# A hybrid attention and recurrence block: the output written feature by feature from the residual tiles, without transposes back

## What is computed

```
h2 = rms_norm(x, norm2_g[l]) * (1.0 + scale2[:, None]) + shift2[:, None]
y = jnp.square(jax.nn.relu(h2 @ w_mlp1[l] + b_mlp1[l])) @ w_mlp2[l] + b_mlp2[l]
x = x + gate2[:, None] * y
return x
```

## Time and profile before

| | |
|---|---|
| median of 3 runs | 888.29 us (887.23 to 888.52) |
| profiled execution, its own time | 887.42 us |
| profiled execution, span from first to last instruction | 885.7 us |
| TensorE busy | 836.6 us, 94% |
| VectorE busy | 461.0 us, 52% |
| ScalarE busy | 332.8 us, 38% |
| GpSimd busy | 222.1 us, 25% |
| mean granted TensorE clock | 0.975 |

### The profile page before, as it was taken

The page is one execution under the profiler, slowest core; times in us unless marked ns, Lnnn a source line. Parts: engine busy times, 40 slices in busy tenths (PEclk is TensorE's granted clock), DMA queues, the critical chain, the costliest instruction groups (busy, mean ns, idle before and its releaser), DMA issues.

```text
span 885.7 us, 10922 instructions
## 1 busy us (share of the span) xinstructions
PE 836.6 (94%) x3951; PEld 673.2 (76%) x3951; DVE 461.0 (52%) x713; ACT 332.8 (38%) x501; POOL 222.1 (25%) x127
## 2 busy tenths in 40 slices
PE   2699899989999999899899989999999999999998
PEld 1567668867878887666688878888888888888886
DVE  3932569995798786574585766952111122220000
ACT  2643434334343326566233234444111144442111
POOL 4023324430000000000000114544444444444440
PEclk9789989999999999899999989999999999999999
DMA  9922312331122222443355732833333333333303
GB/s 357 288 57 73 95 47 72 95 95 48 48 72 55 65 72 73 142 135 103 118 168 163 221 91 70 238 96 95 95 95 95 95 95 95 95 95 115 98 1 95
DMA packets 144554, 95.75 MB, mean 108 GB/s; under 512 B 8198, under 2 KB 138628, under 8 KB 143492
## 3 DMA queue, kind: packets, MB, share of 16 engines
q1 hardware_dynamic: 143104, 95.18, 36.3%
q10 hardware_dynamic: 1412, 0.07, 0.1%
HBM read 93.13 MB, written 2.10 MB: 108 GB/s over the span
## 4 chain that ended last, share of the span: by engine, by line
PE 80%; DVE 13%; ACT 3%; DMA 2%; issue 1%; ACTq 1%; SPq 0%; DVEq 0%
PE bank L1255 16%; PE bank L1256 16%; PE bank L1257 16%; PE bank L1405 3%; PE bank L1407 3%; PE bank L1406 3%; DVE score L967 3%; DVE top L965 2%; PE bank L1425 2%; PE bank L1597 2%; PE bank L1599 2%; PE bank L1598 2%; PE bank L1283 2%; DVE rt_k L927 1%; PE bank L1379 1%
## 5 line engine op out<-in xcount | busy, mean ns | idle before, releaser
L433 POOL TENSOR_TENSOR w_lo<-w_raw,w_hi 128x1024 fp32r<-128x1024 f32 x82 | 203.4, 2482 | 322.6 <-ACT w_hi L504 322.6
L1255 PE MATMUL bank<-h_hi,w_hi 128*128 128x512 f32 x464 | 184.8, 398 | 5.6 <-DVE h_lo L905 5.1
L504 ACT ACTIVATE w_hi<-w_raw 128x1024 fp32r<-128x1024 f32 x126 | 132.5, 1052 | 144.9 <-PE bank L1257 121.4
L1256 PE MATMUL bank<-h_lo,w_hi 128*128 128x512 f32 x464 | 182.5, 393 | 0.0
L1257 PE MATMUL bank<-h_hi,w_lo 128*128 128x512 f32 x464 | 182.5, 393 | 0.0
L1255 PEld LDWEIGHTS bank<-h_hi,w_hi 128*128 128x128 f32 x464 | 88.2, 190 | 29.9 <-issue 8.0
L1257 PEld LDWEIGHTS bank<-h_hi,w_lo 128*128 128x128 f32 x464 | 88.2, 190 | 18.8
L1256 PEld LDWEIGHTS bank<-h_lo,w_hi 128*128 128x128 f32 x464 | 88.3, 190 | 17.9 <-issue 0.2
L1255 PE MATMUL bank<-u_hi,w_hi 128*128 128x512 f32 x256 | 100.0, 391 | 0.0
L1257 PE MATMUL bank<-u_hi,w_lo 128*128 128x512 f32 x256 | 99.7, 389 | 0.0
L1256 PE MATMUL bank<-u_lo,w_hi 128*128 128x512 f32 x256 | 99.6, 389 | 0.0
(11 more groups left out here) (233 smaller groups left out, 1233.3 us busy)
## 6 DMA issues: line engine op xcount, KB each, us to landing
w_raw<-in_w_mlp SPq DMA_DIRECT2D x128, 256.0 KB, 3.0
w_raw<-in_w_in SPq DMA_DIRECT2D x88, 256.0 KB, 3.3
ada_raw<-in_w_ada SPq DMA_DIRECT2D x8, 1024.0 KB, 8.9
ada_even<-in_w_ada SPq DMA_DIRECT2D x16, 512.0 KB, 4.8
ada_odd<-in_w_ada SPq DMA_DIRECT2D x16, 512.0 KB, 4.9
w_raw<-in_w_out SPq DMA_DIRECT2D x16, 256.0 KB, 3.2
x_nat<-in_x SPq DMA_DIRECT2D x4, 512.0 KB, 5.9
w_raw<-in_w_proj_a SPq DMA_DIRECT2D x8, 256.0 KB, 2.9
```

The source lines that it names most:

```text
L433: nc.gpsimd.tensor_tensor(w_lo[:, s], w_raw[:, s], w_hi[:, s].bitcast(F32), ALU.subtract).then_inc(lo_ready, 1)
L504: nc.scalar.activation(w_hi[:, s], w_raw[:, s], ACT.Copy).then_inc(hi_ready, 1)
L1255: mm(bank[b][:], w_hi[:, slot, j], rhs_hi(i), start=f, stop=False)
L1256: mm(bank[b][:], w_hi[:, slot, j], rhs_lo(i), start=False, stop=False)
```

## The change

The output tensor becomes (1024 features, 512 tokens), and the host turns the result. Each tile of `xT` is written straight to its 128 rows of it. `turn_back` goes, with the 32 transposes, the eight copies of ScalarE and `o_stage`. SP waits for VectorE's counts of `lin_evac`. The last tile is done by VectorE in two halves of 256 tokens; SP writes the first half, the queue of ScalarE the second. A row of the output that a write touches is 2 KB long for tiles 0 to 6 and 1 KB for the halves; before it was 512 bytes.

```diff
-    out_v = out[0].rearrange("(b p) (m n) -> m p b n", p=P, n=P)
+    out_v = out.rearrange("(m p) t -> m p t", p=P)
...
-        o_stage = place("o_stage", RL + 8 * KB, [P, 2, TB, P])
...
-        y_turned, out_staged = sem("y_turned"), sem("out_staged")
-        out_written = [sem("out_written0"), sem("out_written1")]
+        out_written, tail_written = sem("out_written"), sem("tail_written")
...
         @block.sync
...
-            for m in range(KC):
-                sp.wait_ge(out_staged, m + 1)
-                sp.dma_start(out_v[m], o_stage[:, m % 2]).then_inc(out_written[m % 2], 16)
-            for b in range(2):
-                sp.wait_ge(out_written[b], 16 * KC // 2)
+            for m in range(KC - 1):
+                sp.wait_ge(lin_evac, E_2[1] + m + 1)
+                sp.dma_start(out_v[m], xT[:, m]).then_inc(out_written, 16)
+            sp.wait_ge(lin_evac, E_2[1] + KC)
+            sp.dma_start(out_v[KC - 1][:, 0:T // 2], xT[:, KC - 1, 0:T // 2]).then_inc(out_written, 16)
+            sp.wait_ge(out_written, 16 * KC)
...
         @block.scalar
...
-            for m in range(KC):
-                act.wait_ge(y_turned, m + 1)
-                if m >= 2:
-                    act.wait_ge(out_written[m % 2], 16 * (m // 2))
-                nc.scalar.activation(o_stage[:, m % 2], bank[2 + m % 2][:].rearrange("p (b n) -> p b n", b=TB),
-                                     ACT.Copy).then_inc(out_staged, 1)
+            act.wait_ge(lin_evac, E_2[1] + KC + 1)
+            act.dma_start(out_v[KC - 1][:, T // 2:T], xT[:, KC - 1, T // 2:T]).then_inc(tail_written, 16)
+            act.wait_ge(tail_written, 16)
...
         @block.vector
...
-                        v.scalar_tensor_tensor(out=xT[:, m], in0=bank[m % 2][:], scalar=GATE2[:, m:m + 1],
-                                               in1=xT[:, m], op0=ALU.mult, op1=ALU.add).then_inc(lin_evac, 1)
+                        for t in ((slice(0, T // 2), slice(T // 2, T)) if m == KC - 1 else (slice(0, T),)):
+                            v.scalar_tensor_tensor(out=xT[:, m, t], in0=bank[m % 2][:, t], scalar=GATE2[:, m:m + 1],
+                                                   in1=xT[:, m, t], op0=ALU.mult, op1=ALU.add
+                                                   ).then_inc(lin_evac, 1)
...
         @block.tensor
...
-            def turn_back(m):
-                pe.wait_ge(lin_evac, E_2[1] + m + 1)
-                if m >= 2:
-                    pe.wait_ge(out_staged, m - 1)
-                for b in range(TB):
-                    end = nc.tensor.transpose(bank[2 + m % 2][:, b * P:(b + 1) * P],
-                                              xT[:, m, b * P:(b + 1) * P], ident[:])
-                end.then_inc(y_turned, 1)
-
-
-            for j in range(4):
-                down(3, (j,))
-                for m in (2 * j, 2 * j + 1):
-                    if m < KC - 2 or j == 3 and m < KC - 1:
-                        turn_back(m)
-            turn_back(KC - 1)
+            down(3)
...
-    out = nc.dram_tensor("out", inputs["x"].shape, F32, kind="ExternalOutput").ap()
+    _, T, D = inputs["x"].shape
+    out = nc.dram_tensor("out", (D, T), F32, kind="ExternalOutput").ap()
     hybrid_block(nc, *args, out)
-    return run_bass_kernel_spmd(nc, [arrays], core_ids=[0]).results[0]["out"]
+    res = run_bass_kernel_spmd(nc, [arrays], core_ids=[0]).results[0]["out"]
+    return np.ascontiguousarray(np.asarray(res).T)[None]
```

## The result

| | before | changed |
|---|---|---|
| median, 15 executions each | 887.54 us (883.09 to 888.66) | 882.30 us (877.77 to 883.59) |
| profiled execution | 887.42 us | 882.97 us |
| its span | 885.7 us | 881.2 us |

The ratio is 0.9945, 95% interval [0.9931, 0.9960]: the kernel got faster by 3.5 to 6.1 us. The sign, the mechanism and the profiled execution (883.0 forecast, 882.97 measured) came as forecast.

What follows compares the result with a forecast made beforehand. TensorE's matmul stream bounds the kernel up to 880.8 us, then a serial tail; 2.7 in the stream, 1.3 hand-overs plus 0.5 write size minus 0.1 halving give 4.4 less, median 883.9 us, stated range 882.9 to 886.0.

Steps and rivals of the forecast that it cites:

- The stream: TensorE's last units: without the three blocks of eight transposes between matmuls, the stream gets 2.7 us shorter.
- The halves of VectorE: Last tile on VectorE: two independent halves overlap by 0.08 and take 0.89 us, where the whole took 0.76.
- What leaves the tail: Behind VectorE's last operation: hand-overs, transposes back and ScalarE's copy go entirely, 1.34 us, and nothing takes their place.
- The write: Last half's write from the ScalarE queue: 128 KB instead of 256 KB lands after 1.8 us, 0.5 off 2.3.
- The early writes and the last load: Seven other writes on SP, behind the last load: priced at 0, as that load has 14.6 us of cover.
- The sum against the profiled execution: Whole kernel: span 881.3 us, 4.4 less, so profiled execution 883.0 against 887.42 before.
- The step that failed: Carrying the sum from the profiled execution over to the median: 888.29 − 4.4 = 883.9 us.
- the bounds 4.7 and 3.6: Most and least total gain in us: 2.7 + 1.34 + 0.6 and 2.6 + 1.34 − 0.31.
- Rival 1: Last tile's write: a half costs as much as a whole one; gain 3.9, time 884.4 us; chance 0.12.
- rival 2: Last half's write: the ScalarE queue is slow, landing takes 2.8 us more; gain 1.6, time 886.7; chance 0.08.
- rival 3: TensorE's edited stretch: matmuls run less densely and the stream gives no time back; 1.7 us remain, 886.6; chance 0.02.
- rival 4: TensorE's last units: clock falls from 2.4 to 1.2 GHz, 10.9 us a unit; two such units give 894.8; chance 0.03.

## Why the prediction was wrong where it was

**The stream (2.7 forecast).** Right. The blocks put back alone cost 2.7 us, in units of 6.35; the changed kernel has none longer than 5.44.

**The halves of VectorE (0.89).** Right: 0.88, with the second starting 0.40 us after the first, as the pair without dependence had it.

**What leaves the tail (1.34).** Right: nothing stands between VectorE and the write.

**The write (0.5 off, 2.3 to 1.8).** The term was right to a tenth (2.3 to 1.7), its reason was half wrong. I put all of it down to size. Size gives 0.3 (2.0 to 1.7), and the fewer and longer pieces give 0.3 (2.3 to 2.0); the two pairs of loads that I drew on (2.7 and 2.1) differed in size and in piece length, and no run shows that the 0.6 between them is size alone. The rule of the Trainium skill ("DMA: Bandwidth & Descriptors", the two cost components), by which the 128 KB less are worth an estimated 0.3 us, agrees with the 0.3 between whole and halved write. The page fits that rule to transfers issued by GpSimd; these are SP's and ScalarE's. It has no term for the 0.3 that the pieces give, so a comparison with my whole 0.5 was not a test of it.

**The early writes and the last load (0).** Right: held back or not, 338.7 from the mark; the last load landed in 3.0.

**The sum against the profiled execution.** 883.0 forecast, 882.97 measured; 4.4 against 4.5 between the spans, 4.56 from the mark. That the time itself agrees to 0.03 us is luck in part: the two profiled executions happen to have nearly the same level (542.45 and 542.53). With a level like that of the kernel whose last tile is undivided (539.15) it would have been 3.4 us less.

**The step that failed is the last one**, where the difference was carried over to the median: "median 888.29 − 4.4 = 883.9", with "its three runs lie within 1.3 us" as the spread. Three runs were not enough to fix a level. The kernel before has a median of 887.54 over the 15 executions beside the changed kernel's, and over its six sets of 12 to 23 executions the medians run from 885.63 to 887.54, while single executions lie between 882.5 and 888.8. The three shown were all from the upper part. Of the 1.6 us by which 882.30 lies under 883.9, 0.75 are that (888.29 to 887.54) and 0.15 the trace's 4.56 against 4.4. The remaining 0.7 are within what medians of one kernel do (1.5 us apart in the kernel before against itself). With 887.54 in place of 888.29 the sum gives 883.1. The range has a slip besides: the bounds 4.7 and 3.6 and half of 1.3 give 882.9 to 885.3, not "883.1 to 885.0"; since the stated range was then widened to 882.9, that did not decide.

Behind the spread stands a cause, not noise without a name. The level is set ahead of the mark, mostly between 98 and 135 us, by how much of the time TensorE is granted 1.2 GHz after two waits of 2 us. Shown: the same program with a clock of 0.86, 0.91 or 1.00 there has its mark at 543.3 to 543.7, 540.7 to 543.3 or 539.1; with the waits filled the clock stays at 1.00, and executions of the changed kernel spread over 2.2 and 2.7 us (six each) instead of 5.8 (fifteen). (A spread over fifteen is wider than one over six in any case; the standard deviations, 0.9 and 2.2 us, say the same.) Not shown is why the unfilled kernel has one or the other in a given execution, nor which levels the three first runs and the two medians had: they were not traced.

Rival 1 (size counts for nothing) is refuted by whole against halved, 2.0 against 1.7; rival 2 by the ScalarE queue's 1.7; rival 3 by the blocks put back; rival 4 by a clock of 1.00 over all edited units. My use of the clock was at the wrong place: I weighed it where the change is, at 860 us, and had the earlier trace rows before me with a clock under 1.00 elsewhere, without asking whether it is the same in each execution.

**Open:** whether the change also moves the level ahead of the mark. Means over all executions of both unedited kernels give 886.28 (102 of before) and 881.39 (27 of the changed one), 4.9 us apart with a standard error of 0.45: 4.56 fits, and 5.2 isn't excluded. No run shows a way by which the change could do it.

## What to carry to other kernels

Work on the engine that is the bound costs its time at the place where it stands, whoever reads the result; if the output can be had in the layout in which the tiles are, the turning is free to go, and with it the hand-overs of the tail. Make the sum against one trace, but fix the level, and the width of the range, by asking how the granted clock differs between executions: three runs that agree within 0.15% may all be from one side. Behind the last matmul count every hand-over first; halving the last tile was worth 0.1 us here, since the second instruction takes half of what the smaller write gains.

## What the runs showed of the hardware

- Waits of TensorE of about 2 us can cost more than themselves: in the same program the window that holds them ran at a granted clock of 0.86 or 0.91 in eleven profiled executions and at 1.00 in two, and the mark moved by over 4 us. Seventeen idle matmuls of 128x128 in these gaps held it at 1.00 in each of the four profiled executions so edited, and brought the changed kernel's median from 0.9945 to 0.9918 of the kernel before. Twenty and ten of them in the waits at 12 and 39 us brought nothing (0.9963).
- A write of 256 KB lands after 2.3 us in pieces of 512 bytes and after 2.0 in pieces of 2 KB; one of 192 KB in pieces of 1.5 KB after 1.9; one of 128 KB in pieces of 1 KB after 1.7 to 1.8; one of 64 KB in pieces of 512 bytes after 1.6, and after 1.8 when issued 0.29 us behind one of 192 KB.
- Matmuls of 128, 256, 384 and 512 columns follow one another after 0.11, 0.12, 0.18 and 0.23 us: from 256 on it goes nearly with the columns, and 128 are hardly cheaper than 256.
- Two operations of VectorE without dependence overlap by 0.08 us.
